# Seven RMS norms of a two-block network: token sums as columns, root on 128x4, result spread by TensorE, idle matmuls, and the unit behind a norm with tiles of h outermost

## What is computed

```python
def rmsnorm(x, w, eps):                                    # over the 1024 features of a token
    return x * lax.rsqrt(jnp.mean(x * x, axis=-1, keepdims=True) + eps) * w

def first_block(x, ...):
    h = rmsnorm(x, norm_mix_w) * (1 + scale_m) + shift_m                # norm 0
    x = x + gate_m * hybrid_mixer(h, ...)
    h = rmsnorm(x, norm_mlp_w) * (1 + scale_f) + shift_f                # norm 1
    x = x + gate_f * (square(relu(h @ w_up)) @ w_down)
    return rmsnorm(x, norm_final_w)                                     # folded: norm 3

def second_block(x, ...):
    h = rms_norm(x, pre_mix_g) * (1 + sc1) + sh1                        # norm 2, on both norms at once
    y = token_mixer(h, ...)
    x = x + g1 * rms_norm(y, post_mix_g)                                # norm 4
    h = rms_norm(x, pre_ffn_g) * (1 + sc2) + sh2                        # norm 5
    y = conv_ffn(h, ...)
    return x + g2 * rms_norm(y, post_ffn_g)                             # norm 6
```

## Time and profile before

| | us |
|---|---|
| median of 3 runs | 1830.14 (1829.32 to 1831.88) |
| profiled execution, its own time | 1830.04 |
| its span, first to last instruction | 1828.1 |
| PE busy | 1676.4 (92%) |
| DVE, POOL, ACT busy | 885.0, 783.9, 633.1 |
| mean granted TensorE clock | 0.958 |

### The profile page before, as it was taken

One profiled execution on the slowest core, in us unless ns is written; L12 is line 12 of the kernel. 1 busy time (PEld: TensorE's weight loads), 2 busy tenths in 40 slices (PEclk: granted clock), 3 DMA queues, 4 the chain that ended last, 5 costly groups with the idle time before them and its releaser, 6 DMA issues.

```text
span 1828.1 us, 20595 instructions
## 1 busy us (share of the span) xinstructions
PE 1676.4 (92%) x7578; PEld 1348.3 (74%) x7578; DVE 885.0 (48%) x1158; ACT 633.1 (35%) x824; POOL 783.9 (43%) x632
## 2 busy tenths in 40 slices
PE   3998999999989999799999997999877799999995
PEld 2677778787768877588888886778755577888884
DVE  5546454545575253644334445474655654113424
ACT  3444434343223222432123222355143433334421
POOL 1273545555345544354444552332242255444441
PEclk7898999999999999899999997999988999999997
DMA  8111122112135535235544441221011132232221
GB/s 319 47 69 47 70 70 93 70 70 92 70 105 183 173 121 196 75 139 177 182 149 150 176 181 72 92 70 47 23 50 66 50 134 101 81 107 93 93 88 61
DMA packets 35234, 194.32 MB, mean 106 GB/s; under 512 B 3904, under 2 KB 4160, under 8 KB 19776
## 3 DMA queue, kind: packets, MB, share of 16 engines
q1 hardware_dynamic: 23616, 151.06, 23.2%
...
## 4 chain that ended last, share of the span: by engine, by line
PE 72%; DVE 13%; POOL 5%; ACT 4%; issue 3%; DMA 2%; DVEq 0%; SPq 0%; ACTq 0%
PE main L738 55%; PE main L734 9%; POOL w_lo L583 5%; ACT w_hi L1041 2%; PE auxB L762 1%; DVE rstd L1640 1%; DVE h_lo L1670 1%; DVE tmp L1578 1%; PE auxD L841 1%; DVE tmp L1435 1%; DMA ada_first<-w_ada 1%; PE auxD L906 1%; DVE tmp L1776 1%; DVE x L1655 1%; DVE ysum L1654 1%
## 5 line engine op out<-in xcount | busy, mean ns | idle before, releaser
L583 POOL TENSOR_TENSOR w_lo<-raw,w_hi 128x512 fp32r<-128x512 f32 (+1 forms) x522 | 695.6, 1364 | 860.2 <-ACT w_hi L1041 860.0
L738 PE MATMUL main<-h_hi,w_hi 128*128 128x512 f32 (+2 forms) x1136 | 456.4, 402 | 31.0 <-DVE h_lo L1670 16.4
L738 PE MATMUL main<-h_lo,w_hi 128*128 128x512 f32 (+2 forms) x1136 | 448.4, 395 | 0.0
L738 PE MATMUL main<-h_hi,w_lo 128*128 128x512 f32 (+2 forms) x1136 | 447.8, 394 | 0.0
L1041 ACT ACTIVATE w_hi<-raw 128x2048 fp32r<-128x2048 f32 (+3 forms) x136 | 247.9, 1823 | 267.3 <-PE main L738 220.0
L738 PEld LDWEIGHTS main<-h_hi,w_hi 128*128 128x128 f32 (+2 forms) x1136 | 214.9, 189 | 97.7 <-issue 21.2
L738 PEld LDWEIGHTS main<-h_hi,w_lo 128*128 128x128 f32 (+2 forms) x1136 | 215.3, 190 | 48.3 <-issue 1.0
L738 PEld LDWEIGHTS main<-h_lo,w_hi 128*128 128x128 f32 (+2 forms) x1136 | 215.5, 190 | 43.7 <-issue 0.5
L1578 DVE SCALAR_TENSOR_TENSOR tmp<-main,par,tmp 128x511 f32<-128x511 f32 x88 | 66.0, 750 | 175.9 <-ACT tmp L1142 174.4
L1603 DVE SCALAR_TENSOR_TENSOR ada_acc<-ada_raw,cs,ada_acc 128x1024 f32<-128x1024 f32 x70 | 115.7, 1653 | 38.2 <-DMA ada_raw<-w_ada 29.2
L734 PE MATMUL main<-w_hi,h_hi 128*128 128x512 f32 (+1 forms) x256 | 103.4, 404 | 14.1 <-DVE h_lo L1670 6.8
...
## 6 DMA issues: line engine op xcount, KB each, us to landing
...
```

The source lines that it names most:

```text
L583: ins = nc.gpsimd.tensor_tensor(w_lo[:, s, a:b], raw[:, s, a:b], w_hi[:, s, a:b], ALU.subtract)
L738: ins = nc.tensor.matmul(bank[0:n, :], w[:, k, col:col + n], a[:, ka_, :], start=start, stop=stop)
```

## The change

1. Sums. `column_sums` takes the squares as the weights and streams one column of ones, so that the sum of each of the 512 tokens lands in one of 4 columns of 128 rows in bank C. In `SPREAD` norms DVE adds only up to tile 6, and tile 7 goes to PE by itself.
2. A new stage `root`: ACT's root and DVE's reciprocal on 128x4. The activation table for it is asked for by a dummy root ahead of the last square.
3. PE spreads: four 128x128 matmuls, with a column of `r_col` as weights broadcast to 128, leave the reciprocal root in bank D, from which DVE reads it (norms 1 to 6). For norm 3 this stands at the unit's end.
4. Idle matmuls (`stay_busy`, 128x128 fp32 of the identity, results unused): 7 between the two column sums, 2 behind them, and behind the spread 9 ahead of a unit or 1 otherwise; 2 behind each tile's sums in norm 5.
5. POOL makes `h_lo` of odd tiles (from a copy with the shift that ACT writes back to `tmp`), and the odd adds to x of norms 4 and 6.
6. The unit behind a norm (`behind_norm`): tile of h outermost, jobs inside, all its banks at once.

```diff
-    before[at["UP"][0]] += square_sums(1, at["OUT"]) + [("norm", 1)]
+    before[at["UP"][0]] += square_sums(1, at["OUT"]) + [("root", 1), ("norm", 1)]
...
-    mid[wo + 1] += [all_sums(3)[-1], ("norm", 3)]
+    mid[wo + 1] += [all_sums(3)[-1], ("root", 3)]
+    end[wo + 1] += [("norm", 3)]
...
+            def norm(i, n):                                   # POOL
+                kind = NORMS[i][3]
+                if kind == "add":
+                    for k in range(1, KD, 2):
+                        pool.wait_ge(norm_ys, (0 if i == 4 else KD // 2) + k // 2 + 1)
+                        nc.gpsimd.tensor_tensor(x[:, k, :], x[:, k, :], ysum[:, k, :], ALU.add).then_inc(x_pool, 1)
+                if kind == "h":
+                    m = split_norms.index(i)
+                    for k in range(1, KD, 2):
+                        pool.wait_ge(norm_id, KD // 2 * m + k // 2 + 1)
+                        nc.gpsimd.tensor_tensor(h_lo[:, k, :], tmp[:, k % 4, :], h_hi[:, k, :],
+                                                ALU.subtract).then_inc(norm_lop, 1)
...
+            def behind_norm(u, wh, wl):
...
+                for k in range(KD):
+                    for a, w in ((h_hi, wh), (h_hi, wl), (h_lo, wh)):
+                        if a is h_lo:
+                            pe.wait_ge(*lo_made(m, k))
+                        elif w is wh:
+                            pe.wait_ge(norm_hi, KD * m + k + 1)
+                        for t in range(u.n_jobs):
...
+            def stay_busy(bank, n):
+                ins = None
+                for _ in range(n):
+                    ins = nc.tensor.matmul(bank[:, 0:P], ident, ident, start=True, stop=True)
+                return ins
+
+            def column_sums(bank, of, first, last):
+                for c in range(TC):
+                    ins = nc.tensor.matmul(bank[:, c:c + 1], of[:, chunk(c)], ones[:, 0:1],
+                                           start=first and c == 0, stop=last and c == TC - 1)
+                return ins
+
+            def norm(i, n):                                   # PE
...
+                pe.wait_ge(norm_root, i)
+                for c in range(TC):
+                    ins = nc.tensor.matmul(bank[:, chunk(c)], r_col[:, c:c + 1].to_broadcast([P, P]), ident, start=True, stop=True)
+                ins.then_inc(full, 1)
+                bank, full = take(("sumsq", sum_stage(i)), 2)
+                if first_unit_after.get(i):
+                    ins = stay_busy(bank, 9)
+                else:
+                    ins = stay_busy(bank, 1)
...
+                        pe.wait_ge(norm_add, (KD - 2) * (SPREAD.index(i) + 1))
+                        column_sums(bank, rstd, True, False)
+                        if i != 3:
+                            stay_busy(room, 7)
+                        pe.wait_ge(norm_sq, SQUARED[i])
+                        column_sums(bank, tmp[:, 1, :], False, True).then_inc(full, 1)
+                        if i != 3:
+                            stay_busy(room, 2)
...
+                    if k == KD - 1 and i in (1, 2, 4, 6):     # ACT
+                        run_act(small[:, 21:22], ones[:, 0:1], ACT.Sqrt)
...
+                link(run_act(root, bank[:, 0:TC], ACT.Sqrt, bias=NORM_EPS_OF[i], scale=1.0 / D_MODEL))
...
+                nc.vector.reciprocal(r_col, root).then_inc(norm_root, 1)
```

More of the change, by code:

```diff
@@ L501, in build, with added, lo_made @@
         Y_AT = {4: 8, 6: 24}
+        SQUARED = [8, 16, 24, 32, 40, 48, 56]
+        def added(i, k):
+            before_it = 0 if i == 4 else KD // 2
+            return (x_pool, before_it + k // 2 + 1) if k % 2 else (x_ready, 4 * KD + before_it + k // 2 + 1)
+        def lo_made(m, k):
+            return (norm_lop if k % 2 else norm_lo), KD // 2 * m + k // 2 + 1
+        root, r_col = small[:, 52:56], small[:, 56:60]
         split_norms = [n for n, v in enumerate(NORMS) if v[3] == "h"]
@@ L666, in _ @@
                 run(sorted(end[u.n], key=xdt_first))
+            run(last)
         @block.tensor
@@ L741, in project @@
                 return ins
+            def behind_norm(u, wh, wl):
+                m = sum(1 for v in split_norms if first_unit_after[v] < u.n)
+                for t in range(u.n_jobs):
+                    j = u.job0 + t
+                    if j >= 4:
+                        pe.wait_ge(main_free[j % 4], j // 4)
+                for k in range(KD):
[4 more added lines that the diff above has]
+                            pe.wait_ge(norm_hi, KD * m + k + 1)
+                        for t in range(u.n_jobs):
+                            j = u.job0 + t
+                            bank = main[j % 4]
+                            start, stop = k == 0 and w is wh and a is h_hi, k == KD - 1 and a is h_lo
+                            if u.token_major:
+                                ins = nc.tensor.matmul(bank[:, 0:u.cols], a[:, k, chunk(t)], w[:, k, :], start=start, stop=stop)
+                            else:
+                                n = min(P, u.cols)
+                                ins = nc.tensor.matmul(bank[0:n, :], w[:, k, P * t:P * t + n], a[:, k, :], start=start, stop=stop)
+                            if stop:
+                                ins.then_inc(main_full[j % 4], 1)
+                return ins
@@ L743, in sumsq @@
             def sumsq(item, n):
                 i, pair = item
+                if i in SPREAD:
+                    if item == sum_stage(i):
+                        bank, full = take(("sumsq", item), 0)
+                        room, _ = take(("sumsq", item), 1)
+                        pe.wait_ge(norm_add, (KD - 2) * (SPREAD.index(i) + 1))
[6 more added lines that the diff above has]
+                            stay_busy(room, 2)
+                    return
@@ new lines, in sumsq @@
+                if i == 5:
+                    if pair == 0:
+                        take(("sumsq", item), 0)
+                        take(("sumsq", item), 1)
+                    for k in range(2 * pair, 2 * pair + 2):
+                        pe.wait_ge(norm_sq, KD * i + k + 1)
+                        ins = column_sums(aux["C"], tmp[:, k % 4, :], k == 0, k == KD - 1)
+                        ins.then_inc(norm_use if k < KD - 1 else aux_full["C"], 1)
+                        stay_busy(aux["D"], 2)
+                    return
@@ L745, in sumsq @@
                 if item == sum_stage(i):
                     bank, full = take(("sumsq", item), 0)
-                    if i in SPREAD:
-                        pe.wait_ge(norm_add, (KD - 1) * (SPREAD.index(i) + 1))
-                        nc.tensor.matmul(bank[:, :], ones, rstd[:, :], start=True, stop=True).then_inc(full, 1)
-                if i in SPREAD:
-                    return
                 for k in range(2 * pair, 2 * pair + 2):
@@ L1177, in sumsq @@
                         act.wait_ge(x_in_sem, 16)
+                    elif i == 5:
+                        act.wait_ge(*added(4, k))
                     elif src == "x":
@@ L1632, in sumsq @@
                 if i in SPREAD:
-                    for k in range(max(1, 2 * pair), 2 * pair + 2):
+                    for k in range(max(1, 2 * pair), min(KD - 1, 2 * pair + 2)):
                         dve.wait_ge(norm_sq, KD * i + k + 1)
@@ L1660, in norm @@
                         dve.wait_ge(*units_over(first_unit_after[i]))
[L1661 to L1667 removed]
+                    for k in range(KD):
+                        if k >= 4:
+                            dve.wait_ge(*lo_made(m, k - 4))
+                        stt(tmp[:, k % 4, :], x[:, k, :], scale[:, k:k + 1], r[:, :], ALU.mult,
+                            ALU.mult).then_inc(norm_tmp, 1)
+                        if k % 2:
                             dve.wait_ge(norm_hi, KD * m + k)
                             dve.wait_ge(norm_tmp, KD * m + k)
[L1670 removed]
+                            stt(h_lo[:, k - 1, :], tmp[:, (k - 1) % 4, :], shift[:, k - 1:k], h_hi[:, k - 1, :],
                                 ALU.add, ALU.subtract).then_inc(norm_lo, 1)
+                    if i:
+                        dve.wait_ge(norm_tmp, KD * (m + 1))
+                        dve.sem_inc(free, 1)
             def dt_turn(i, n):
```

88 lines of the change are left out of this document (53 added, 35 removed).

## The result

| | before | after |
|---|---|---|
| runs, median (lowest to highest), us | 1830.04 (1829.32 to 1831.88) | 1849.14 (1845.64 to 1854.49) |
| profiled execution, own time, us | 1830.04 | 1845.64 |

The changed kernel is slower: ratio 1.010, 95% interval 1.0086 to 1.0114, some 19 us. The forecast was 1850. The other 3.5 have no row here; that they lie in where the clock falls is likely and not shown (the mean granted clock is 0.961 in the execution of 1845.6 us and 0.957 in that of 1854.5).

What follows compares the result with a forecast made beforehand. PE was taken to bound the kernel (72% of the chain, DVE 13%). The terms 6.7 + 2.3 + 0.9 - 3.9 + 2.0 + 10.6 + 0 + 1.5 = +20.1 on 1830.04 gave 1850 us, range 1824 to 1857.

Steps and rivals of the forecast that it cites:

- Norm 0, POOL's queue: Start of X0: POOL's four h_lo pieces ahead of w_lo delay it to 66.3, +6.7 us; clock drop +2.3.
- Norm 5: Norms 4 and 5: sums and idle matmuls at half clock, 2.68 us a tile; FU+1 10.6 us later.
- 3.6 to the first square: Norm 5: its sums start 3.6 us after norm 4's first tmp, at 1416.1.
- Which clock: Norm chains: the clock falls to 0.50 where it fell before; norm 1's first tmp comes 1.6 us later.
- the full-clock case: Norm 1 at full clock: first tmp 1.6 us earlier, -2.3 us in all instead of +0.9.
- The units behind: Behind norms 1, 2 and 5: next unit starts 18.3, 17.7 and 17.4 us after the norm's first tmp.
- tiles outermost pays at KV alone: Units behind norms: POOL's w_lo is late next, so this order pays only where PE was late before, KV.
- the w_lo waits can drop the clock: PE's waits behind UP, KV and FU, about 3 us each: up to 2.3 us each, +1.5 together.
- Norm 6: First tmp +2.0 us at half clock or -1.3 at full, adds -0.4; taken as 0.
- The 25 ns a matmul of the Trainium skill: Column sums on PE: eight records would cost 0.2 us, forecast several us lower; set aside for the trace's 115 ns.
- idle matmuls hold the clock: Rival: clock stays at 1.0 through each norm, about -9 us, 1821; chance 0.17.

Runs made afterwards that it cites:

- experiment 1: The changed kernel with POOL's w_lo of X0 moved back ahead of norm 0's h_lo pieces; ratio 1.0077 to the kernel before.
- experiment 11: The changed kernel without idle matmuls, X0's w_lo first on POOL, norm 5's bank D taken late, and all h_lo on DVE; ratio 0.9958 to the kernel before.
- experiment 3: The changed kernel with norm 5's idle matmuls written to bank C, so that bank D is taken only for the spread; ratio 1.0063 to the kernel before.
- experiment 2: The changed kernel without the two idle matmuls behind each tile's sums in norm 5; ratio 1.0074 to the kernel before.
- experiment 4: The changed kernel with norm 5 alone summed and rooted on 512 columns as before the change, without idle matmuls between; ratio 1.0043 to the kernel before.
- experiment 7: The changed kernel with X0's w_lo ahead of norm 0's h_lo pieces on POOL and norm 5 on 512 columns; ratio 1.0005 to the kernel before.
- experiment 6: The changed kernel with the four jobs outermost again in the units behind norms 0, 1, 2 and 5; ratio 1.0136 to the kernel before.
- Experiment 5: The changed kernel without its idle matmuls, except one behind each spread that signals the bank; ratio 1.0026 to the kernel before.

## Why the prediction was right

The sign, the size (1850 forecast, 1849.1 measured) and the main terms were right. That it was hit to 1 us is luck: the terms add up to 20.1 us and the stretches of the profiled execution to 15.6, with errors of both signs among them, and the median lies 3.5 us above that execution for reasons that no term held.

- *Norm 0, POOL's queue*: 66.3 forecast for X0, 66.06 measured, and experiment 1 gives 4.7 of the 6.4 us to the order of the queue. The blocking of DVE and POOL is in there too, 2.5 us less 1.3 that other parts of the change give back (experiment 11). The clock was at 0.50 for 6.9 us at X0, but PE was idle for the first 3; 3.85 us of matmuls ran at half, which cost 1.9 us, instead of 2.3.
- *Norm 5*: the largest term. Half clock throughout and 2.56 us a tile instead of 2.68 were as forecast. The step that failed is the count from norm 4's T0 to the first sum, "3.6 to the first square": it was 9.24 us (1413.05 to 1422.29), because I had costed the idle matmuls and not the bank that they write. With the bank taken late the first sum came after 3.46 us (experiment 3). So T4 to T5 was 31.8 us and not 26.8. Experiments 2, 3 and 4 take 6.0, 6.5 and 14.5 us of it away.
- *Which clock*: I took it to fall wherever it fell before. It did so in norm 5 and from the middle of norm 4's chain on, only for 3.4 us in norm 2, and not at all in the sums of norms 1, 3 and 6 as profiled. There T1 came 1.67 us earlier against the last add, the value of the full-clock case. This is the step that was too simple: with the idle matmuls in place the clock of one and the same chain holds in one execution and falls in another (experiment 7). Whether they make the times spread more is not shown: the changed kernel's four lie 9 us apart and the four of the kernel before 2.6, but its 15 to 20 runs beside the experiments lie 8 to 10 us apart.
- *The units behind*: 17.01, 16.57 and 16.56 us behind T0 where 18.3, 17.7 and 17.4 were forecast. A pair of tiles took DVE 2.3 us instead of the 2.5 of the forecast (tmp at 750.27, 752.63 and 754.89), and POOL's w_lo behind norm 1 took 5.40 us instead of 5.93. That w_lo ends last there and that tiles outermost pays at KV alone was right and is shown by the rows and experiment 6. That the w_lo waits can drop the clock was right too, but priced too low: 3.4 us at 0.50 behind each of UP+1, QA0 and FU+1, so 1.7 lost each and 5.1 together, where the sum has 1.5. It does not happen every time: in experiment 1 PE waited 2.98 us at QA0, and no 0.50 stretch followed.
- *Norm 6*: 0 forecast; T6 came 1.1 us earlier against its last add that both kernels have (6.25 us instead of 7.39), at the full clock, and T6 to the end took 13.39 us instead of 13.65 (forecast 0.4 less).
- *The 25 ns a matmul of the Trainium skill* (TensorE: Matmul & The Clock Gate, section "Wait — 56ns, not 53.3ns?"): the page gives it as the least start-to-start. As a price it does not fit: the column sums ran at 0.12 us a record at full and 0.213 at half in the changed kernel too.

Of the rivals, "idle matmuls hold the clock" was true in norm 1's profiled chain and still worth only -2 there. Experiment 5 decides it for the whole kernel: without them the time is 13 us lower, 5 of it in norm 5 by experiment 2. Whether POOL's add beside DVE's costs or gains anything in norm 4 was not tried alone.
